# The recurrent mixer's scan state is scaled and copied by VectorE instead of ScalarE

## What is computed

```python
def wkv_scan(s0, scan_in):
    def step(s, inp):
        w, kk, a, k, v, r = inp
        sa = jnp.einsum('dbhij,dbhj->dbhi', s, kk)
        s = s * w[..., None, :] - sa[..., :, None] * (kk * a)[..., None, :] + v[..., :, None] * k[..., None, :]
        return s, jnp.einsum('dbhij,dbhj->dbhi', s, r)
    return lax.scan(step, s0, scan_in)
...
    s0 = jnp.zeros((2, B, RW_HEADS, RW_HEAD, RW_HEAD), jnp.float32)
    s_ctx, y_c = wkv_scan(s0, scan_c)
    _, y_x = wkv_scan(s_ctx, scan_x)
    o_bx = rwkv_post(from_scan(y_x), *aux_x, rw_g_up, rw_r_k, rw_ln_g, rw_ln_b)
```

## Time and profile before

| what | value |
| --- | --- |
| time, median of 3 runs | 4470.25 us (4462.68 to 4473.83) |
| the profiled execution: time, span | 4473.57 us, 4471.9 us |
| granted TensorE clock, mean over the span | 0.962 |
| busy share of the span | TensorE 89%, VectorE 63%, ScalarE 34%, GpSimd 19% |
| recurrent mixer | about 2080 to 2850 us of the span |

### The profile page before, as it was taken

One profiled execution on the slowest core, in us unless ns is written; L12 is line 12 of the kernel. 1 busy time (PEld: TensorE's weight loads), 2 busy tenths in 40 slices (PEclk: granted clock), 3 DMA queues, 4 the chain that ended last, 5 costly groups with the idle time before them and its releaser, 6 DMA issues. The chain is left out here.

```text
span 4471.9 us, 74705 instructions
## 1 busy us (share of the span) xinstructions
PE 3989.3 (89%) x29550; PEld 2820.5 (63%) x29550; DVE 2817.3 (63%) x5982; ACT 1521.7 (34%) x3304; POOL 866.4 (19%) x908
## 2 busy tenths in 40 slices
PE   7989999988999899998999999898999777787787
PEld 6747887755788787786877788687444333333333
DVE  5674433765533476755766766335777888888885
ACT  3353342343523335713555555333111111111111
POOL 1101110110201101100000000000344444454443
PEclk9999999999999899999999999899999999999988
DMA  4203443311543310231000000333999999999998
GB/s 127 84 26 112 153 139 98 107 31 38 163 143 118 116 57 20 79 118 49 17 18 20 18 30 6 129 113 133 396 405 416 417 419 406 415 413 412 411 408 336
DMA packets 150606, 795.18 MB, mean 178 GB/s; under 512 B 19897, under 2 KB 23209, under 8 KB 83441
## 3 DMA queue, kind: packets, MB, share of 16 engines
q0 software_dynamic: 84496, 574.75, 31.9%
q1 hardware_dynamic: 58272, 188.32, 13.0%
q10 hardware_dynamic: 7488, 27.30, 1.8%
HBM read 766.11 MB, written 20.00 MB: 176 GB/s over the span
## 5 line engine op out<-in xcount | busy, mean ns | idle before, releaser
L3189 PE MATMUL psum<-rows,diag 128*128 128x512 f32 x2048 | 995.1, 636 | 239.4 <-ACT diag L3068 224.7
L3189 PEld LDWEIGHTS psum<-rows,diag 128*128 128x128 f32 x2048 | 406.5, 204 | 784.3 <-issue 771.3
L2930 DVE SCALAR_TENSOR_TENSOR uh<-rows,h_rows 128x1024 f32<-128x1024 f32 x512 | 627.7, 1226 | 208.2 <-DMA rows<-in_peer_uv,sel_idx 182.2
L2887 POOL DMA_INDIRECT rows<-in_peer_uv,sel_idx x512 | 613.2, 1198 | 737.6 <-PE psum L3189 675.8
L529 DVE TENSOR_TENSOR w_split_lo<-w_raw,w_split_hi 128x1024 fp32r<-128x1024 f32 (+1 forms) x271 | 326.3, 1214 | 494.9 <-ACT w_split_hi L516 490.4
L516 ACT CAST w_split_hi<-w_raw 128x1024 fp32r<-128x1024 f32 (+1 forms) x271 | 276.4, 1028 | 615.3 <-PE psum L465 394.7
L3061 ACT ACTIVATE g<-g 128x4 f32<-128x4 f32 x128 | 26.3, 205 | 1091.7 <-DVE g L2941 1091.7
L693 POOL TENSOR_TENSOR uT_lo<-normed_rows,uT_hi 128x512 fp32r<-128x512 f32 x64 | 90.0, 1407 | 668.5 <-ACT uT_hi L669 668.5
L465 PE MATMUL psum<-hT_mlp_hi,w_split_hi 128*128 128x512 f32 x512 | 200.5, 392 | 4.7 <-DVE hT_mlp_lo L261 4.5
L465 PE MATMUL psum<-hT_mlp_lo,w_split_hi 128*128 128x512 f32 x512 | 199.8, 390 | 0.0
L465 PE MATMUL psum<-hT_mlp_hi,w_split_lo 128*128 128x512 f32 x512 | 199.7, 390 | 0.0
(11 more groups left out here) (526 smaller groups left out, 8635.4 us busy)
## 6 DMA issues: line engine op xcount, KB each, us to landing
w_raw<-in_w_in SPq DMA_DIRECT2D x105, 512.0 KB, 4.1
w_raw<-in_w_up SPq DMA_DIRECT2D x64, 512.0 KB, 4.1
w_raw<-in_w_down SPq DMA_DIRECT2D x64, 512.0 KB, 4.5
amask_sb<-in_w_mod ACTq DMA_DIRECT2D x48, 512.0 KB, 4.8
wq<-in_peer_wq SPq DMA_DIRECT2D x24, 512.0 KB, 7.9
rows<-in_peer_uv,sel_idx POOLq DMA_INDIRECT x512, 12.8
qkpad<-in_w_out SPq DMA_DIRECT2D x12, 512.0 KB, 4.8
w_raw<-in_w_out SPq DMA_DIRECT2D x12, 512.0 KB, 4.2
```

The source lines that it names most:

```text
L2887: nc.gpsimd.indirect_dma_start(out=rows[:, n % RB, :], out_offset=None, in_=I["peer_uv"], in_offset=bass.IndirectOffsetOnAxis(ap=sel[:, t, ...
L2930: nc.vector.scalar_tensor_tensor(prod[:], rows[:, n % RB, 0:D], 1.0, h[:, t, :], ALU.mult, ALU.mult, accum_out=dots[:, (n // BATCH) % 2, s ...
L3189: last = nc.tensor.matmul(psum[:, 2 * (t % 2) + half, :], diag[:, n % (2 * BATCH), :], rows[:, n % RB, D + half * NB:D + (half + 1) * NB], ...
```

## The change

ScalarE's `scan` loses its branch for slot 3n+2. VectorE gets a function `state`, called in slots 2, 5, ... 32 between its `solve` and its `turn` of the slot. It reads the same PSUM bank, multiplies by the same column of `pl` and writes the same buffer. In place of ScalarE's wait for `pl_ready` (VectorE makes `pl` itself) it waits for `y_done`, that is for the readers of the buffer; before the change ScalarE's copy of N, earlier in the same queue, had done that waiting. Number of instructions, PSUM layout and TensorE's program are unchanged.

```diff
--- before.py
+++ after.py
@@ -2274,12 +2274,6 @@
                     elif n == 0 and u:
                         act.wait_ge(y_done, 8 * u)
                     nc.scalar.copy(Nn[:], psum[:, 4, L_CH:2 * L_CH]).then_inc(n_copied, 1)
-                elif n < NCH - 1:
-                    if n == 0:
-                        act.wait_ge(pl_ready, u + 1)
-                    act.wait_ge(s_ready, 11 * u + n + 1)
-                    nc.scalar.activation(Ss[:, (n + 1) % 2], psum[:, 5, 0:L_CH], ACT.Copy, scale=pl[:, u % 3, c:c + 1]
-                                         ).then_inc(s_copied, 1)
 
             def open_lora(k, u):
                 w, half = divmod(k // 2, 2)
@@ -2373,6 +2367,17 @@
 
         @block.vector
         def _(dve):
+            def state(n, u):
+
+                c = orders[u % 2][n]
+                if n == 0 and u:
+                    dve.wait_ge(y_done, 8 * u)
+                elif n > CCH:
+                    dve.wait_ge(y_done, 8 * u + n - CCH)
+                dve.wait_ge(s_ready, 11 * u + n + 1)
+                nc.vector.tensor_scalar(Ss[:, (n + 1) % 2], psum[:, 5, 0:L_CH], pl[:, u % 3, c:c + 1], None, ALU.mult
+                                        ).then_inc(s_copied, 1)
+
             def solve(k, u):
                 d = u % 2
                 if k < 3:
@@ -2538,6 +2543,8 @@
                 for k in range(SLOTS_):
                     if build is not None:
                         solve(k, build)
+                    if scanned is not None and k % 3 == 2 and k < SLOTS_ - 1:
+                        state(k // 3, scanned)
                     if build is not None:
                         turn(k, build)
                         if 3 <= k < 12:
```

## The result

The changed kernel takes 4501.94 us (median of 4 runs, 4496.75 to 4507.11) against 4467.24 (4462.68 to 4473.83) for the kernel before: ratio 1.0076, 95% interval 1.0058 to 1.0093. It is slower by 35 us. The profiled execution has a span of 4505.5 us, 33.6 more.

What follows compares the result with a forecast made beforehand. TensorE, 92% busy, was taken to set the mixer's pace. Even iterations 21, odd 25, two others 3 and squares 2 summed to +51 us: 4524 from the profiled time, 4521 against the runs, range 4487 to 4567.

Steps and rivals of the forecast that it cites:

- the last scan: End of the recurrent mixer: the last scan runs with VectorE nearly idle, so it adds 0 us.
- Price: One S copy on VectorE: 0.28 us taken, between 0.22 and 0.34, against 0.31 us on ScalarE.
- The walk: Slot by slot in one even and one odd iteration: copy placed behind its VectorE predecessor, compared with TensorE's time of need.
- the prediction's own 80 terms: Some 40 late copies and as many queued ones, each moved 0.06 us by the price's ends: -5 and +5 us.
- Even iterations: Recurrent mixer: six even iterations with the norm lose 3.5 us each through late S copies, 21 us.
- the walked one: The even iteration from 2364 to 2410 us, building unit 6 and scanning unit 5: TensorE falls 3.5 us behind.
- The slot 29 wait: Even iterations: VectorE's copy waits for S's products, pushing the reciprocals behind it; slot 32's copy then loses 2.5 us.
- Odd iterations: Recurrent mixer: seven odd iterations with the layer norm lose 3.6 us each, at slots 14, 23, 26 and 32, 25 us.
- slot 23's comparison: Odd iteration: copy behind the second reciprocal lets TensorE on at 2446.75 against its need at 2445.25, 1.5 us lost.
- 2 us for the squares: Slot 14, seven odd iterations: VectorE's 0.28 us ahead of squares for which TensorE already stands adds 2 us.
- fall behind for good: Rival, mixer: copy and masked copies feed each other's lag, about 4566 us, up to 4600; chance 0.11.
- ScalarE's relief: Rival, mixer: TensorE's 4.8 us stand for S goes, kt and W copies come earlier; -18, about 4452 us; chance 0.07.

Runs made afterwards that it cites:

- the kernel with a stand of 1.19 us from the second reciprocal: Changed kernel with the first norm reciprocal called ahead of slot 29's S copy instead of behind it: 4489.04 us, ratio 1.0045.
- the one with the six late slots: VectorE copies S only in slots 2, 14, 17, 23, 26 and 32 (96 of 176), ScalarE in the others: 4492.30 us, ratio 1.0061.
- the one with 2.2 us: Changed kernel with a second multiply of the same PSUM columns in front of each S copy, into a spare tile: 4521.25 us, ratio 1.0118.
- the two where that stand is gone or 0.27 us: Changed kernel with both norm reciprocals and the odd iterations' layer-norm reciprocal moved, 4475.33 us; changed kernel with only the second norm reciprocal behind slot 32's copy, 4488.79 us.

## Why the prediction was right, and where its sizes were off

Forecast +51 us (4521), measured +35 (4502), with the sign and the mechanism as walked. The size is too high, most of all in the odd iterations, and two things that I had put at nothing, the clock and the last scan, hide part of that.

**Price.** 0.28 us taken, 279 ns measured on the way to TensorE. By the Trainium skill's table (VectorE: DVE Perf Modes, section on the TRN2 errata) it would have been 0.19, an estimate; the measured duration, of a copy scaled by a column, doesn't agree. In the queue, though, a copy costs 0.19 to 0.20 us, since the next instruction starts before its end. The Trainium skill's page Perfetto Trace Analysis (Optimizing Scalar/DVE Operations) says that the write-acknowledgement of one instruction overlaps with the next, and the rows at 2400.01 and 2400.20 agree. The walk used 0.28 for both, and whole durations for the predecessors: about 0.1 us too much at each late copy, more where several queue up. That is also why VectorE's busy share rose to 70% and not to 76%: its busy time in the steady part grew by 26.5 us for 163 more instructions, 0.16 each, because an overlap counts once. (By the prediction's own 80 terms, 0.19 in place of 0.28 would take 7 us off its sum, not 5.)

**Even iterations.** From one slot-32 need to the next, before and after. TensorE's timeline of the kernel before, units scanned one earlier and one later than in the earlier trace rows:

```profile
2360.58 0.33 PE L1937 MATMUL psum<-S_cells,qr 64*64 64x64 f32 x4
...
2454.01 0.33 PE L1937 MATMUL psum<-S_cells,qr 64*64 64x64 f32 x4
```

and of the changed kernel, one need more:

```profile
2320.37 0.33 PE L1937 MATMUL psum<-S_cells,qr 64*64 64x64 f32 x4 [1.87 <-DVE S_cells L2378]
...
2368.42 0.33 PE L1937 MATMUL psum<-S_cells,qr 64*64 64x64 f32 x4
...
2466.61 0.33 PE L1937 MATMUL psum<-S_cells,qr 64*64 64x64 f32 x4
```

The even iteration took 2407.07 - 2360.58 = 46.49 us and takes 2416.93 - 2368.42 = 48.51: +2.0 where I walked to +3.5; the six have +2.0 to +2.9, 14.8 us together where the sum had 21. In the walked one TensorE loses, from need to need, 0.15 at slot 2 (walked 0.3), 0.9 at slot 14 (1.2), 0.8 at slot 17 (1.1) and 1.9 at slot 32 (2.5): the stands, and 0.15 each for the part of the last product that the stand doesn't count. It gets back 2.2 by slot 26 (1.6), and loses 0.5 at slot 29, behind its new stand for the norm's root, which the walk left out.

The walked iteration also isn't like the other five. Before the change kr ended 1.5 us behind slot 17's need there, and 0.4 to 0.7 behind it in the others; and a stand as long as 0.82 us before slot 23's need is in that iteration alone. In the other five slot 17 costs 0.1 to 0.2 us, though kr still waits for the DMA in all six (18.2 us, 19.1 before). Multiplying one iteration by six was the error there.

The slot 29 wait was a smaller cause than I said. I made it the start of the whole 2.5 us; the runs give it 0.7 of 1.88 us of stand, and 1.19 to the second reciprocal, which stands in front of slot 32's copy whether or not the first is pushed.

**Odd iterations.** 2454.01 - 2407.07 = 46.94 us before, 2466.61 - 2416.93 = 49.68 after: +2.7 where I walked to +3.6. But 1.6 of that is clock (last section). The odd iteration before it kept the clock and takes 2368.42 - 2320.37 = 48.05, against 46.94 for the same one before the change: the copies cost +1.1, less than a third of the walk. This is the term that was most wrong: 7 x 1.1 = 8 us in place of 25. Slots 14, 23 and 26 stand 0.86, 0.99 and 1.34, 3.2 us together and near the walk's 3.5. But I took TensorE's other stands as untouched. The kernel before stood for VectorE's squares 6.6 us and for its masked copies

```profile
PE psum L1937 <- DVE x L2403: 6.6, 12, 0.6
```

and both are gone from the waits after: having lost time at slot 14 or 26, TensorE finds the squares and masked copies ready. What slot 14 costs is given back by slot 17. The walk carried its 1.1 us to the end, without having raised either side of slot 23's comparison by it. It added 2 us for the squares, where 6.6 came off, and left the other 6.6 in place.

**The whole.** Over all releasers the stands of the waits views add up so: S +35.0, the norm's root +2.7, W -2.1, squares -6.6, masked copies -6.6, the rest -1.3; that is +21. There are 86 pieces where there were 72, and 14 x 0.15 us that the brackets leave out are 2; the clock takes 6. The sum is 29, and by as much the part from 2140 us to the end of the last build has grown (670 to 699). The last scan, which I put at 0, takes 29.0 us instead of 26.8 between its slot-32 need and the one before, and with it the 31 us of the stretch are complete. What makes it longer was not taken apart.

**The clock.** I wrote 1.00 and named a fall as a sign of being wrong; it fell four times in the steady part. These 6 us and the 2 of the last scan are no part of the walk, so some 8 of the measured 35 us came nearer to the forecast by luck. Without them the time would be some 27 us above the one before, still in the range.

**The rivals.** VectorE doesn't fall behind for good: the same pieces return in each iteration, so there is no growing lag. ScalarE's relief gave little: kt's stand is 15.7 us in every kernel, and W's went from 11.4 to 9.3, which no run takes apart.

**What isn't settled.** Slot 14's stand in odd iterations was not taken apart. Why the clock falls behind some stands of a length and not behind others is open.

## What to carry to other kernels

Before moving a small link of a dependence chain to another engine, don't compare durations or busy shares: put it behind its predecessor in that engine's order, slot by slot, and compare with the time at which the next engine wants it. Long operations that filled a gap are the danger twice, once in front of the copy and once when the copy's own wait pushes them. A stand removed or added seldom counts in full, since the same engine's next stands shrink or grow against it: sum the waits view over all releasers, not one. And look at the granted clock before taking a difference for stands: two iterations with the same stands differed by 1.6 us here. One iteration, however carefully walked, may not stand for its kind: compare its length with the others first.

## What the runs showed of the hardware

Behind some of TensorE's stands the granted clock falls. TensorE's timeline of the changed kernel behind slot 32's stand, at the end of an iteration that kept the clock and of one that didn't (same instructions):

```profile
2322.61 1.13 PE L2167 MATMUL psum<-lora,arena 128*128 128x512 f32 x2
...
2323.67 1.09 PE L1937 MATMUL psum<-qr,arena 64*64 64x128 f32 x16
...
2419.16 1.90 PE L2167 MATMUL psum<-lora,arena 128*128 128x512 f32 x2
...
2420.99 1.95 PE L1937 MATMUL psum<-qr,arena 64*64 64x128 f32 x16
```

The lora product takes 1.13 us in one and 1.90 in the other, and 16 Gram products 1.09 in one and 1.95 in the other. The windows view above gives the granted clock of the two stretches as 1.00 and 0.66, that is a part of the second at 1.2 instead of 2.4 GHz. In the changed kernel this follows four of six stands of 1.88 us before slot 32's need. From that need to the next iteration's slot 2 TensorE then takes 9.0 us (8.5 in one case) where it takes 7.4 with the clock kept: 1.6 us more (1.1 in that case), 6 in all. It is more frequent behind longer stands: in the kernel with a stand of 1.19 us from the second reciprocal it follows two of six, in the one with the six late slots one of six, in the one with 2.2 us all six, and in the two where that stand is gone or 0.27 us, none. The steady part of the kernel before has none.
